# Adaptive-layer-norm columns: transposes of the copied rows and a sum of four strips on VectorE, in place of products with a picking matrix

## The reference

```python
silu_c = jax.nn.silu(c)
silu_cc = jax.nn.silu(c_ctx)[None, :]
for i in range(DEPTH):
    mx = jnp.split((silu_c @ ada_w[i] + ada_b[i])[:, None, :], 6, axis=-1)
    mc = jnp.split((silu_cc @ ada_w[i] + ada_b[i])[:, None, :], 6, axis=-1)
    hx = modulate_norm(xs, norm_mix[i], mx[0], mx[1])
    hc = modulate_norm(cs, norm_mix[i], mc[0], mc[1])
    yx, yc = mixer(hx, hc)        # neighbourhood attention, retention, convolution, attention
    xs = xs + mx[2] * yx
    xs = xs + mx[5] * conv_ffn(modulate_norm(xs, norm_ffn[i], mx[3], mx[4]), ...)
    # the same for cs with mc, in all layers but the last
```

## Time and profile before

| what | value |
|---|---|
| median of 3 runs | 2739.63 us (2738.41 to 2741.62) |
| the profiled execution, its own time | 2741.23 us |
| its span, first to last instruction | 2739.4 us |
| mean granted TensorE clock | 0.984 of full speed |
| TensorE busy | 2642.6 us, 96% of the span |
| VectorE busy | 1470.9 us, 54% |
| ScalarE busy | 914.9 us, 33% |
| GpSimd busy | 264.8 us, 10% |

### The profile page before, as it was taken

The page is one execution under the profiler, slowest core; times in us unless marked ns, Lnnn a source line. Parts: engine busy times, 40 slices in busy tenths (PEclk is TensorE's granted clock), DMA queues, the critical chain, the costliest instruction groups (busy, mean ns, idle before and its releaser), DMA issues. The chain is left out here.

```text
span 2739.4 us, 38756 instructions
## 1 busy us (share of the span) xinstructions
PE 2642.6 (96%) x13988; PEld 2146.3 (78%) x13988; DVE 1470.9 (54%) x2199; ACT 914.9 (33%) x1443; POOL 264.8 (10%) x252
## 2 busy tenths in 40 slices
PE   6899999999999999999999998999999999999999
PEld 4677787777788866788777887878777788778999
DVE  3765645454245344426454328867545425946774
ACT  2225622222122123313222216544222223335443
POOL 5100030000110020030000110003000013102000
PEclk8999999999999999999999999989999999999999
DMA  8431035544423321323544322112444434311455
GB/s 264 160 121 39 0 123 178 177 152 175 154 85 100 109 75 47 115 97 136 176 153 174 125 91 70 52 57 87 172 175 174 152 100 118 113 62 47 160 182 179
DMA packets 95022, 337.38 MB, mean 123 GB/s; under 512 B 11984, under 2 KB 13776, under 8 KB 94800
## 3 DMA queue, kind: packets, MB, share of 16 engines
q1 hardware_dynamic: 90320, 324.28, 34.6%
q0 software_dynamic: 2880, 8.92, 1.6%
q10 hardware_dynamic: 1728, 2.85, 0.3%
HBM read 334.95 MB, written 1.05 MB: 123 GB/s over the span
## 5 line engine op out<-in xcount | busy, mean ns | idle before, releaser
L553 PE MATMUL bank<-Hhi,Whi 128*128 128x512 f32 (+1 forms) x2440 | 885.4, 363 | 37.0 <-DVE Hlo L1338 15.5
L554 PE MATMUL bank<-Hlo,Whi 128*128 128x512 f32 (+1 forms) x2440 | 863.9, 354 | 0.0
L555 PE MATMUL bank<-Hhi,Wlo 128*128 128x512 f32 (+1 forms) x2440 | 862.9, 354 | 0.0
L1284 DVE TENSOR_TENSOR Wlo<-raw,Whi 128x1024 fp32r<-128x1024 f32 x424 | 530.1, 1251 | 393.8 <-ACT Whi L1007 392.0
L1007 ACT ACTIVATE Whi<-raw 128x1024 fp32r<-128x1024 f32 x424 | 447.5, 1057 | 866.2 <-DMA raw<-in_weights 865.7
L553 PEld LDWEIGHTS bank<-Hhi,Whi 128*128 128x128 f32 x2440 | 467.2, 191 | 138.5 <-issue 60.7
L554 PEld LDWEIGHTS bank<-Hlo,Whi 128*128 128x128 f32 x2440 | 467.2, 191 | 63.2 <-issue 4.6
L555 PEld LDWEIGHTS bank<-Hhi,Wlo 128*128 128x128 f32 x2440 | 466.6, 191 | 63.2
L553 PE MATMUL bank<-Ghi,Whi 128*128 128x512 f32 (+1 forms) x770 | 269.7, 350 | 0.0
L555 PE MATMUL bank<-Ghi,Wlo 128*128 128x512 f32 (+1 forms) x770 | 267.4, 347 | 0.0
L554 PE MATMUL bank<-Glo,Whi 128*128 128x512 f32 (+1 forms) x770 | 266.0, 345 | 0.0
(11 more groups left out here) (193 smaller groups left out, 2911.0 us busy)
## 6 DMA issues: line engine op xcount, KB each, us to landing
raw<-in_weights SPq DMA_DIRECT2D x424, 512.0 KB, 3.3
ada_ring<-in_ada SPq DMA_DIRECT2D x176, 512.0 KB, 5.7
ada_raw<-in_ada SPq DMA_DIRECT2D x16, 512.0 KB, 16.0
rel_in<-in_rpb POOLq DMA_DIRECT2D x48, 128.0 KB, 4.5
decay_t<-in_dist POOLq DMA_DIRECT2D x4, 640.0 KB, 4.2
X<-in_x ACTq DMA_DIRECT2D x1, 2048.0 KB, 9.6
out_y<-X SPq DMA_DIRECT2D x1, 1024.0 KB, 4.8
cos_sin<-in_rope ACTq DMA_DIRECT2D x1, 256.0 KB, 13.7
```

What stands on the lines that cost most here:

```text
L553: t.matmul(dst, Whi[:, st.slot, w], hi, start=start, stop=False)
L554: t.matmul(dst, Whi[:, st.slot, w], lo, start=False, stop=False)
L555: return t.matmul(dst, Wlo[:, st.slot, w], hi, start=False, stop=stop)
L1284: v.tensor_tensor(Wlo[:, st.slot, :], raw[:, st.slot, :], Whi[:, st.slot, :].bitcast(F32), ALU.subtract)\
```

## The change

`ada_cols` no longer multiplies by the picking matrix. It transposes the four 128x128 blocks of `rows` (with the identity that the attention's transposes use), and so fills all 512 columns of bank 7: block q's columns 128q to 128q+127 hold the 128 row numbers of `rows`, of which 0, 1, 32, 33, 64, 65, 96 and 97 are of use. `ada_store` then adds the four strips with a reduction on DVE into a new tile `ada_sum` (128 x 4 x 2), waits for that on a new semaphore, and adds the bias from there. The constant `picker` and its transfer go.

```diff
-        picker = sb("picker", [P, 2])
+        ada_sum = sb("ada_sum", [P, 4, 2])
...
+        strips_added = sem("strips_added")
...
-        FIRST_CONSTS = [(ada_bias, bias_ada), (pick, picker), (ones, one), (identity, ident)]
+        FIRST_CONSTS = [(ada_bias, bias_ada), (ones, one), (identity, ident)]
...
                 for q in range(4):
-                    last = t.matmul(bank[7][:, 2 * q:2 * q + 2], rows[:, P * q:P * q + P], picker[:, :],
-                                    start=True, stop=True)
+                    last = t.transpose(bank[7][:, P * q:P * q + P], rows[:, P * q:P * q + P], ident[:, :])
                 last.then_inc(cols_made, 1)
...
                 dve.wait_ge(cols_made, index + 1)
-                v.tensor_tensor(mod_slices[:, bass.ts(index - earlier, 4), :],
-                                bank[7][:, 0:8].rearrange("p (q s) -> p q s", s=2),
+                strips = bank[7][:, :].rearrange("p (q j r) -> p q r j", j=4, r=QUAD)[:, :, 0:2, :]
+                v.tensor_reduce(ada_sum[:, :, :], strips, axis=AX, op=ALU.add).then_inc(strips_added, 1)
+                dve.wait_ge(strips_added, index + 1)
+                v.tensor_tensor(mod_slices[:, bass.ts(index - earlier, 4), :], ada_sum[:, :, :],
                                 bias_slices[:, bass.ts(index, 4)].unsqueeze(2).to_broadcast([P, 4, 2]), ALU.add)\
                     .then_inc(mod_ready, 1)
```

More of the change, by code:

```diff
@@ L146, in build @@
 def build(nc, x, ada, weights, ada_in, ada_bias, gain, na_gain, rpb, na_mask, rope, decay, dist, gn_gain,
-          cv_bias, cv_filter, ffn_filter, ones, head_ones, identity, pick, out):
+          cv_bias, cv_filter, ffn_filter, ones, head_ones, identity, out):
     layers, n_groups = plan()
@@ L1818, in _constants @@
         "identity": np.eye(P, dtype=np.float32),
-        "pick": np.tile(np.eye(QUAD, 2, dtype=np.float32), (4, 1)),
     }
```

## The result

| | before | after |
|---|---|---|
| median of 4 runs each, us | 2740.62 (2738.41 to 2741.79) | 2707.07 (2704.26 to 2714.99) |
| the profiled execution: own time, span, clock | 2741.23, 2739.4, 0.984 | 2714.99, 2713.2, 0.985 |

The ratio is 0.9883, interval 0.986 to 0.9906: faster by 33.6 us at the medians, where 16.3 was predicted, and outside the range. The profiled execution of after is the slowest of its four; between the two profiled executions the difference is 26.2 us.

What follows compares the result with a forecast made beforehand. TensorE was taken to bound the laps. Savings of 15.5 us (42 groups), 0.5 (slice 4) and 0.6 (prologue), less 0.3 (slice 7), gave 16.3 us: 2739.6 - 16.3 = 2723.3 us, range 2718 to 2732.

Steps and rivals of the forecast that it cites:

- VectorE's work is hidden: In up laps, VectorE's added 0.3 us a slice falls in 2.24 us of idle time, so nobody waits for it.
- layer 3 does not change: Sign in the profile after: layer 3 has no slices and should keep its length.
- 192 records: Rival at the groups: transposes keep two records each, 0.89 us a group, 2743 us in all; chance 3%.
- laps that keep what they save: Rival: later waits give TensorE's lap saving back, in the extreme half of 15.5 us, 2731 to 2738 us; chance 7%.
- clock 1.00: Rival: TensorE falls to half clock behind each group, 2770 us or 2955 us by length of spell; chance 3%.
- a reduction of 184 ns: Rival: VectorE's two instructions are far dearer, over 2 us, and TensorE's tiles wait, 2750 us; chance 1%.
- The group's saving: At 42 groups, four transposes at 0.44 us replace 0.81 us, saving 0.37 us each, 15.5 us in all.
- the sum: All terms: 15.5 + 0.5 + 0.6 - 0.3 = 16.3 us saved, giving 2723.3 us against the median.
- The lower bound of the price: For the new group: four times the old record's pitch, 0.40 us, a saving of 0.41 us.
- The spread of the runs: Runs before were taken to spread by 1 to 2 us either way, in setting the range 2718 to 2732 us.
- Slice 4: Group at half clock in the query and key products: 0.5 us saved, between 0.37 and 0.84.
- VectorE at slice 7: Behind slice 7, VectorE's chain gets 0.3 us longer uncovered; TensorE's wait grows from 4.5 to about 5.2 us.

Runs made afterwards that it cites:

- e3: After with every group's four transposes issued twice, eight in all; median 2738.29 us, ratio 0.9994 to before.
- e10: Before with two picking products a group instead of four, leaving out two of the four blocks of each slice; median 2714.08 us, ratio 0.9908 to before.
- e1: Before run again with no edit; median 2734.96 us over 12 runs, ratio 0.9988 to the runs of before beside it.
- e2: After run again with no edit; median 2709.97 us over 6 runs, ratio 0.9903 to before.
- e8: After with GpSimd's second mask addition of layer 0 held until slice 4's rows are copied; median 2715.13 us, ratio 0.9911 to before.
- e9: Before with the new form in slices 10 to 47 only, picker kept and sums in an existing tile; median 2724.47 us, ratio 0.9931 to before.
- e12: After, GpSimd held as in e8, and layer 0's fourth-lap ada_store put ahead of the third lap's norm work; median 2707.5 us, ratio 0.9885 to before.
- e11: After without the sum over the strips, only the first strip taken; median 2721.99 us, ratio 0.9932 to before.
- e7: Before with GpSimd's second mask addition of layer 0 held until slice 4's rows are copied; median 2735.37 us, ratio 0.9984 to before.

## Why the prediction was too small

The mechanism was right: TensorE is the bound in the laps, records halve, the clock stays, VectorE's work is hidden, slice 7 gives a little back, layer 3 does not change (436.8 and 437.2 us from the last product of layer 2's down projection to the last of its own). None of the four rivals happened: 192 records, laps that keep what they save, clock 1.00, a reduction of 184 ns. The sizes were off, by the prediction's own steps:

- **The group's saving, the term of the sum that was mis-sized.** "It saves 0.81 - 0.44 = 0.37 us" subtracts prices that are not of the same kind. The old group's 0.81 was the time to the start of a float32r product, and leaves out the 0.09 us by which that product then holds up the next (0.32 for 0.23). The new group's 0.44 came from four transposes in front of a float32 product, and was whole. From start to start in the laps the new group is 0.35 and not 0.44; whole, the two are 0.90 and 0.44. Either way the saving is 0.45 to 0.46 and not 0.37: 42 x 0.08 = 3.4 us. The records fit it: n of them take 0.11 n in all, and 0.11 n less about 0.09 to the product's start (eight: 0.79; measured 0.81 and, in e3, 0.79; four: 0.35; measured 0.35 and, in e10, 0.37). The lower bound of the price, 0.40, was four times 0.10 us a record, from the same short 0.81, and with it the range.
- **The spread of the runs, the step that moved the median furthest.** "The runs before spread by 1 to 2 us either way" came from three runs. The 81 later ones go from 2729.99 to 2749.44 us, in two clusters, and before's median (2740.62) was near the upper one, while after's four had the highest mean clock of all, 0.987. With the group's saving put right the sum gives 19.7 us and 2719.9, inside the range; what is beyond that is this and the terms below.
- **Slice 4.** 0.5 was taken; it is 1.96 us from slice 4 to 5. The group itself gave 0.82, the upper end; the other 1.1 lie behind it. e3, with eight transposes and so no shorter group, also has 29.41 us there, and the stretch differs as much between executions of one kernel: 31.37 and 29.97 in before and e1, 29.41 and 27.88 in after and e2. So the 1.1 are not shown to be the change's.
- **Not in the sum:** 0.37 us at the end of each of three down projections, where 81 products of 256 columns follow each other at 0.1133 us on average, not 0.1178. The profiles of after, e2, e8, e9 and e12 have it; those with eight records a group, e3 among them, and e10 do not, and e11 has it in two layers of three. What makes it is open; 1.1 us.
- **VectorE at slice 7:** 0.44 for 0.3, and the wait 5.42 for the expected 5.2. The net there is -0.2, as good as predicted.

At equal clock the change is then worth 21.7 ± 1.8 us, with 18.9 from the 42 groups. That is 5.4 more than predicted. The three pairs of profiled executions are further apart (26.2 for before and after, 26.7 for e1 and e2, 27.4 for e7 and e8), with clocks within 0.001 of each other, so 21.7 may be somewhat low. The 33.6 us at the medians are more still. Ten runs of after had a mean clock of 0.9866, the 69 of before 0.9841; 0.0025 at 3.1 us for each 0.001 is 7.8 us, and before's median lies in its upper cluster. Without the clock taken out, the means of after's ten runs and of the 81 of before are 29.3 us apart. The same laps ran at 0.9833 in e9 and 0.9837 in e11, whose medians (2724.47, 2721.99) are near the predicted 2723.3. So the last 8 to 12 us are not shown to follow from the change's two parts: that the median fell outside the range was in good part chance, so far as these runs tell. Whether the shift of everything behind the early slices raises the mean clock of just this program, or so few runs can't tell, stays open.

## What to carry to other kernels

Price a short group of instructions by the time that its stretch takes with it, and read one start beyond its successor: the group that goes and the one that comes must stand in front of the same kind of successor, or a part of the price (here 0.09 us, a fifth of the saving) is counted on one side alone. Count records, not columns: here four records cost the same with four columns and with 128. And before a few microseconds are put down to an edit, look at the granted clock of every run and at where the large tiles lie: here a tile of 32 bytes was worth 5 to 7 us and a difference of 0.0025 in mean clock went with 8.

## What the runs showed that was not expected

- Ghi and Glo 32 bytes further on: the down projections' products at a pitch of 0.233 us in place of 0.229; 33.75 for 33.19 us between slices. Layer 1's output projection has both pitches in executions of one kernel (0.2334 in before, 0.2292 in e1).
- A GpSimd addition of 128x3072 held a VectorE instruction that reads several SBUF tiles until its own end, 6.7 us (the split 7.05 for 1.22 us; line 1338 at 55.37 us in before 6.78 for 0.48), but a reciprocal beside it took its usual 3.34 us (e7, at 79.96).
- Half-clock spells come in some executions and not in others of kernels with the same code around them. The one in e12's first lap cost 26.01 - 24.35 = 1.66 us.
